# Blending the two softmax maps of a differential head before the transpose

## The reference, cut to what matters

```
def probs(qf, kf):
    s = einsum('bhqd,bhkd->bhqk', q_block, kf) * scale
    return softmax(where(mask, s, -inf), axis=-1)

a = probs(q1, k1) - lam * probs(q2, k2)
out = einsum('bhqk,bhkv->bhqv', a, v)
diff = rms_norm(out, diff_subln_g) * (1.0 - lam_init)
```

## The time and the profile before

| | us |
|---|---|
| median of three runs | 1382.27 (1382.13 to 1384.47) |
| the profiled execution, time | 1386.45 |
| the profiled execution, span | 1384.7 |
| TensorE busy | 1294.9 (94%) |
| VectorE busy | 844.6 (61%) |
| ScalarE busy | 648.8 (47%) |
| GpSimd busy | 145.3 (10%) |

### The profile page before, as it was taken

The page is one execution under the profiler, slowest core; times in us unless marked ns, Lnnn a source line. Parts: engine busy times, 40 slices in busy tenths (PEclk is TensorE's granted clock), DMA queues, the critical chain, the costliest instruction groups (busy, mean ns, idle before and its releaser), DMA issues.

```text
span 1384.7 us, 17635 instructions
## 1 busy us (share of the span) xinstructions
PE 1294.9 (94%) x6496; PEld 1084.3 (78%) x6496; DVE 844.6 (61%) x1011; ACT 648.8 (47%) x937; POOL 145.3 (10%) x161
## 2 busy tenths in 40 slices
PE   6979799999897989999997998999999999899997
PEld 5868688888686868888886887777899778688886
DVE  4588765455556896545445654667665586555454
ACT  4455454444344563544444253465564754444443
POOL 2927000000057430000000000000000000000000
PEclk9999999999988999999998989999999999999999
DMA  6512346556243314555553354233324445354551
GB/s 219 185 61 93 122 167 220 195 192 203 77 182 120 119 52 154 212 183 190 195 191 131 142 193 157 91 137 110 122 105 168 143 162 198 146 218 182 184 203 53
DMA packets 33683, 213.75 MB, mean 154 GB/s; under 512 B 4272, under 2 KB 6320, under 8 KB 9296
## 3 DMA queue, kind: packets, MB, share of 16 engines
q1 hardware_dynamic: 33552, 212.73, 43.0%
q0 software_dynamic: 64, 0.13, 0.0%
HBM read 211.80 MB, written 1.05 MB: 154 GB/s over the span
## 4 chain that ended last, share of the span: by engine, by line
PE 79%; DVE 12%; ACT 3%; issue 3%; POOL 2%; DMA 0%; DVEq 0%; SPq 0%; ACTq 0%; POOLq 0%; another core or an unknown queue 0%
PE bank L529 22%; PE bank L530 22%; PE bank L531 22%; PE bank L833 3%; DVE wlo L1472 2%; PE bank L642 2%; PE bank L610 2%; PE bank L560 1%; PE bank L629 1%; DVE index L1560 1%; ACT whi L1054 1%; PE bank L702 1%; DVE probs L1596 1%; PE bank L940 1%; POOL gain L453 1%
## 5 line engine op out<-in xcount | busy, mean ns | idle before, releaser
L1472 DVE TENSOR_TENSOR wlo<-raw,whi 128x2048 fp32r<-128x2048 f32 (+2 forms) x202 | 448.8, 2228 | 257.2 <-ACT whi L1054 255.7
L529 PE MATMUL bank<-whi,hT_hi 128*128 128x512 f32 (+2 forms) x1064 | 428.8, 403 | 20.7 <-DVE hT_lo L1496 14.3
L1054 ACT ACTIVATE whi<-raw 128x2048 fp32r<-128x2048 f32 (+2 forms) x202 | 370.7, 1842 | 114.9 <-PE bank L531 112.9
L530 PE MATMUL bank<-wlo,hT_hi 128*128 128x512 f32 (+2 forms) x1064 | 419.5, 394 | 0.0
L531 PE MATMUL bank<-whi,hT_lo 128*128 128x512 f32 (+2 forms) x1064 | 419.0, 394 | 0.0
L529 PEld LDWEIGHTS bank<-whi,hT_hi 128*128 128x128 f32 x1064 | 207.9, 195 | 66.4 <-issue 14.9
L531 PEld LDWEIGHTS bank<-whi,hT_lo 128*128 128x128 f32 x1064 | 207.6, 195 | 43.0
L530 PEld LDWEIGHTS bank<-wlo,hT_hi 128*128 128x128 f32 x1064 | 208.0, 195 | 39.0
L529 PE MATMUL bank<-whi,ffT_hi 128*128 128x512 f32 x240 | 93.7, 390 | 0.0
L531 PE MATMUL bank<-whi,ffT_lo 128*128 128x512 f32 x240 | 93.5, 390 | 0.0
L530 PE MATMUL bank<-wlo,ffT_hi 128*128 128x512 f32 x240 | 93.4, 389 | 0.0
(11 more groups left out here) (243 smaller groups left out, 1419.0 us busy)
## 6 DMA issues: line engine op xcount, KB each, us to landing
raw<-in_ff_loop SPq DMA_DIRECT2D x90, 1024.0 KB, 4.7
raw<-in_w_groups SPq DMA_DIRECT2D x77, 1024.0 KB, 4.8
raw<-in_w_out SPq DMA_DIRECT2D x8, 1024.0 KB, 4.7
raw<-in_ff_first SPq DMA_DIRECT2D x6, 1024.0 KB, 4.7
raw<-in_w_comp SPq DMA_DIRECT2D x4, 1024.0 KB, 4.7
raw<-in_ff_last SPq DMA_DIRECT2D x3, 1024.0 KB, 6.7
raw<-in_next_first SPq DMA_DIRECT2D x4, 512.0 KB, 3.7
raw<-in_next_first SPq DMA_DIRECT2D x2, 1024.0 KB, 4.7
```

Source lines behind the costliest of these rows:

```text
L529: eng.matmul(out, lhsT=hi, rhs=wh, start=start, stop=False)
L530: eng.matmul(out, lhsT=hi, rhs=wl, start=False, stop=False)
L1054: eng.activation(whi[j][:, 0:n], raw[j][:, 0:n], ACT.Copy).then_inc(hi_ready, 1)
L1472: eng.tensor_tensor(wlo[j][:, 0:n], raw[j][:, 0:n], whi[j][:, 0:n].bitcast(F32), ALU.subtract).then_inc(lo_ready, 1)
```

## The change

VectorE now combines the even and the odd map of each head into one map, before the transpose. It multiplies the odd map with the coefficient (even sum) x (-lam) / (odd sum) and adds the even map, which leaves the division by the even sum for the output. Only the combined map is transposed (6 tiles instead of 12) and multiplied with the values (6 tile products instead of 12), all into bank 5. ScalarE copies one bank of transposed maps instead of two, VectorE half a bank instead of one. The output needs one scaling instruction of 512 elements instead of four of 256 and a subtraction. `lam` is negated once a layer by one more small instruction.

TensorE's two waits for `o_done` ahead of `turn_heads` go, since bank 6 isn't written by the values any more. The transposes of a differential group no longer wait for the exponentials but for the new semaphore `blended`, which VectorE raises twice a group.

In this diff `blend`, the shown `blend_copy` and `diff_out` are VectorE's, `blend_turn` and `blend_values` TensorE's; ScalarE's own `blend_copy` is a copy of 512 columns after the first four tiles of a group's transposes.

```diff
+        coef = sb("coef", [P, 4])
+        blended = sem("blended")
...
+            def blend_turn(A, d):
+                eng.wait_ge(blended, 2 * d + 1)
+                for n in range(2):
+                    mm = eng.transpose(bank[2][:, n * P:(n + 1) * P], probs[:, 0, n * P:(n + 1) * P], ident[:, :])
+                eng.wait_ge(blended, 2 * d + 2)
+                for kt in range(2):
+                    for n in range(2):
+                        c = n * SEQ + kt * P
+                        out = bank[2][:, (2 + n) * P:(3 + n) * P] if kt == 0 else bank[3][:, n * P:(n + 1) * P]
+                        mm = eng.transpose(out, probs[:, 1, c:c + P], ident[:, :])
+                    mm.then_inc(pT_ready, 2 - kt)
+            def blend_values(A, c0):
+                eng.wait_ge(pT_act, 2 * A + 4)
+                eng.wait_ge(pT_dve, A + 2)
+                eng.wait_ge(o_done, A + 2)
+                for r in range(RT):
+                    for n in range(2):
+                        v = c0 + n * P
+                        for kt in range(r + 1):
+                            b = 2 * (r + kt) + n
+                            mm = eng.matmul(bank[5][:, (2 * r + n) * P:(2 * r + n + 1) * P],
+                                            lhsT=probsT[:, b // 4, b % 4 * P:(b % 4 + 1) * P],
+                                            rhs=z[:, kt, v:v + P], start=(kt == 0), stop=(kt == r))
+                mm.then_inc(pv_ready, 1)
...
-                attend_turn(A)
+                blend_turn(A, 2 * l)
...
-                attend_turn(A + 1)
-                eng.wait_ge(o_done, A + 3)
+                blend_turn(A + 1, 2 * l + 1)
                 turn_heads(l, 4, zcols(MQ), 4)
...
+            def blend(A, par):
+                eng.wait_ge(exped, 3 * A + 3)
+                dve(eng.reciprocal(inv[:, :], sums[:, par, :]))
+                dve.wait(eng)
+                even, odd = (a[:, :].rearrange("p (n two) -> p n two", two=2)[:, :, i] for i, a in ((0, sums[:, par]), (1, inv)))
+                dve(eng.scalar_tensor_tensor(out=coef[:, :], in0=even, scalar=lam[:, 0:1], in1=odd, op0=ALU.mult,
+                                             op1=ALU.mult))
+                dve.wait(eng)
+                for r in range(RT):
+                    for n in range(2):
+                        if r == 0:
+                            p, q = (probs[:, 0, (2 * n + i) * P:(2 * n + i + 1) * P] for i in range(2))
+                            out = probs[:, 0, n * P:(n + 1) * P]
+                        else:
+                            p, q = (probs[:, 1 + i, n * SEQ:(n + 1) * SEQ] for i in range(2))
+                            out = p
+                        c = 2 * r + n
+                        ins = eng.scalar_tensor_tensor(out=out, in0=q, scalar=coef[:, c:c + 1], in1=p, op0=ALU.mult,
+                                                       op1=ALU.add)
+                        if n:
+                            ins.then_inc(blended, 1)
+                        else:
+                            dve(ins)
+                            if r == 0:
+                                dve.wait(eng)
+            def blend_copy(A):
+                eng.wait_ge(pT_ready, 3 * A + 3)
+                eng.wait_ge(pv_ready, A + 1)
+                eng.tensor_copy(probsT[:, 1, 0:2 * P], bank[3][:, 0:2 * P]).then_inc(pT_dve, 1)
+            def diff_out(A):
+                eng.wait_ge(pv_ready, A + 2)
+                W = 2 * HD
+                eng.tensor_tensor(scr[:, 0, :].rearrange("p (n d) -> p n d", d=W),
+                                  bank[5][:, :].rearrange("p (n d) -> p n d", d=W),
+                                  inv[:, :].rearrange("p (n two) -> p n two", two=2)[:, :, 0:1].to_broadcast([P, 4, W]),
+                                  ALU.mult).then_inc(o_done, 1)
+                eng.wait_ge(o_done, A + 3)
...
-                lo(6, 0); copy_z1(t0, 5, MQ); lo(6, 1)
-                attend_copy(A)
+                lo(6, 0)
+                blend(A, 0)
+                copy_z1(t0, 5, MQ); lo(6, 1)
+                blend_copy(A)
...
-                diff_out(A, 0); diff_norm(l, 0)
+                diff_out(A); diff_norm(l, 0)
+                blend(A + 1, 1)
                 copy_z1(t0, 6, SQ); lo(7, 1)
-                attend_copy(A + 1)
+                blend_copy(A + 1)
```

More of the change, by code:

```diff
@@ L638, in attend_values @@
                     for h in range(4):
-                        out = bank[5][:, (4 * r + h) * dv:(4 * r + h + 1) * dv] if dv == HD else \
-                            bank[5 + r][:, h * dv:(h + 1) * dv]
+                        out = bank[5][:, (4 * r + h) * dv:(4 * r + h + 1) * dv]
                         for kt in range(r + 1):
@@ L779, in _ @@
                 attend_scores(A + 2, lambda h: T_MQ + h // 2, lambda h: T_MK + h // 2)
-                attend_values(A + 1, lambda kt, h: z[:, kt, DV + (2 + h // 2) * 2 * HD:DV + (3 + h // 2) * 2 * HD], 2 * HD)
+                blend_values(A + 1, DV + 2 * P)
                 project(7, 1)
                 attend_turn(A + 2)
-                eng.wait_ge(o_done, A + 4)
                 turn_heads(l, 5, zcols(SQ), 4)
@@ L1131, in attend_copy @@
                     eng.activation(probsT[:, u, :], bank[2 + u][:, :], ACT.Copy).then_inc(pT_act, 1)
+            def blend_copy(A):
+                eng.wait_ge(pT_ready, 3 * A + 2)
+                eng.wait_ge(pv_ready, A + 1)
+                eng.activation(probsT[:, 0, :], bank[2][:, :], ACT.Copy).then_inc(pT_act, 2)
             def diff_stats(l, i):
@@ L1534, in lambda_value @@
                 dve.wait(eng)
+                dve(eng.tensor_scalar(lam[:, 0:1], lam[:, 0:1], -1.0, None, ALU.mult))
+                dve.wait(eng)
             def head_sums(l, s):
@@ L1619, in attend_out @@
                         dve(ins)
-            def diff_out(A, par):
-                eng.wait_ge(pv_ready, A + 2)
+            def blend(A, par):
+                eng.wait_ge(exped, 3 * A + 3)
                 dve(eng.reciprocal(inv[:, :], sums[:, par, :]))
                 dve.wait(eng)
-                odd = inv[:, :].rearrange("p (n two) -> p n two", two=2)[:, :, 1:2]
-                dve(eng.tensor_scalar(odd, odd, lam[:, 0:1], None, ALU.mult))
+                even, odd = (a[:, :].rearrange("p (n two) -> p n two", two=2)[:, :, i] for i, a in ((0, sums[:, par]), (1, inv)))
+                dve(eng.scalar_tensor_tensor(out=coef[:, :], in0=even, scalar=lam[:, 0:1], in1=odd, op0=ALU.mult,
+                                             op1=ALU.mult))
@@ L1628, in diff_out @@
                 dve.wait(eng)
-                W = 2 * HD
                 for r in range(RT):
[L1631 to L1638, removed]
+                    for n in range(2):
[10 more added lines that the diff above has]
+                            ins.then_inc(blended, 1)
@@ L1639, in diff_out, with blend_copy @@
                         else:
                             dve(ins)
-                dve.wait(eng)
-                dve(eng.tensor_tensor(scr[:, 0, :], scr[:, 0, :], scr[:, 1, :], ALU.subtract))
-                dve.wait(eng)
+                            if r == 0:
+                                dve.wait(eng)
+            def blend_copy(A):
+                eng.wait_ge(pT_ready, 3 * A + 3)
+                eng.wait_ge(pv_ready, A + 1)
+                eng.tensor_copy(probsT[:, 1, 0:2 * P], bank[3][:, 0:2 * P]).then_inc(pT_dve, 1)
@@ L1773, in _ @@
                 attend_mask(A + 2, causal)
-                diff_out(A + 1, 1)
+                diff_out(A + 1)
                 attend_copy(A + 2)
```

2 lines of the change are left out of this document (1 added, 1 removed).

## The result

| | before | after |
|---|---|---|
| median of 5 runs of each, us | 1384.47 (1382.13 to 1389.08) | 1398.57 (1397.06 to 1400.86) |
| profiled execution, us | 1386.45 | 1398.18 |
| its span, us | 1384.7 | 1396.4 |
| mean granted clock of TensorE | 0.963 | 0.956 |
| TensorE busy, us | 1294.9 | 1295.8 |

The ratio is 1.0105, 95% interval 1.008 to 1.0129: the kernel is slower, by about twice as much as I forecast, and the time lies above my range (1384.5 to 1393.8). The direction and the place are as predicted, one term is not.

What follows compares the result with a forecast made beforehand. TensorE and VectorE were both taken to be near their limit, handing work to each other. Waits +3.3, clock falls +3.3 and GpSimd collision +1.1 gave +7.7 us on the median 1382.27: 1390.0 us, range 1384.5 to 1393.8.

Steps and rivals of the forecast that it cites:

- The direction and the place: Slower, at 82%; from group A's scores to the mixed rows' transposes (L560), longer by 2 to 5 us a layer.
- The first blend's second signal: Group A, layer 0: VectorE's signal for four of six transposes, at 104.85 us; projection 6 then starts +2.38 us.
- VectorE waits for the transposes of A+2: Behind the second blend VectorE, late before, becomes early and waits some 2 us for TensorE's transposes.
- VectorE's own sum: Both differential groups: blends add 3.9 us, output and copies save 5.2, so -1.3 us a layer.
- The half throughput rule: Rival, 3%: the blends' instructions with two non-bfloat16 SBUF sources run at half throughput, 3.2 us more, 1393.2 us.
- My terms without the clock: TensorE's waits for the two blends, +1.66 us a layer (+3.3 in all), and the GpSimd collision, +1.1 in all.
- The full collision: At `lo(7, 0)`, behind GpSimd's L459: up to 1.1 us lost; half taken in two layers, +1.1 in all.
- I count one fall a layer: TensorE's clock falls behind the A+1 pause only: 3.3 us at half speed lose 1.65 a layer, +3.3 in all.
- the 3.3 us that I had read at 838: Fall in the profile before: after 2.45 us of waiting at 838, clock at 0.53 for some 3.3 us.
- the first pause: TensorE's wait for group A's blend, about 3.3 us (101.5 to 105.0) with two transposes in it; no fall counted.
- The rival: The clock falls in both pauses of a layer: +6.6 us for the falls, +11 in all, 1393.3 us; chance 14%.
- the zero: Base of the forecast: the difference was put on the median of 1382.27 us, not the profiled execution's 1386.45.

Runs made afterwards that it cites:

- fill_both: The kernel after, with TensorE filling its waits for the blends of groups A (16) and A+1 (30) with transposes of the identity; ratio 1.0032 to before, 1390.21 us.
- early_both2: The kernel after, blend of A ahead of `lo(6, 0)`, blend of A+1 behind A's output but ahead of `lo(7, 0)` and the norm; ratio 0.9971 to before, 1382.29 us.
- early2_fill: early_both2 with 36 transposes of the identity in TensorE's wait ahead of the mixed rows; ratio 0.9987 to before, 1384.61 us.
- fill_first: The kernel after with only the wait of group A filled, with 16 transposes of the identity; ratio 1.0092 to before, 1398.4 us.
- early_a: The kernel after with only the blend of group A moved, ahead of `lo(6, 0)`; ratio 1.0036 to before, 1389.76 us.

## Why the prediction was wrong, point by point

**Right: what waits for what.** TensorE waits for the blend four times, and the other engines follow as I wrote. The first blend's second signal was predicted for 104.85; the transposes behind it start at 105.70, less 0.8 and the 0.13 of the way 104.77. VectorE waits for the transposes of A+2 (2.94 us; I said some 2), and the wait of 4.34 us ahead of the mixed rows is as it was: both engines were moved by the same amount.

**Right: VectorE's instructions.** Blend to next instruction: 105.56 - 103.62 = 1.94 and 127.24 - 125.29 = 1.95, predicted 1.96. The output takes 122.48 - 121.77 = 0.71, predicted 0.72. VectorE's own sum is 3.89 - (3.47 - 0.71) - (2.67 - 0.71) - 0.53 for the copies = -1.4 us a layer, predicted -1.3. The half throughput rule of the Trainium skill ("Vector Engine (DVE) Microarchitecture Reference", section 7) is denied by this trace: the four instructions with two float32 sources in SBUF, 768 elements in all, take 1.53 us.

**Right: waits and GpSimd.** My terms without the clock were 1.66 a layer and half of 1.1, 4.4 us in all; without falls of the clock fill_both measured 2.39 and 2.30 a layer and 0.32% of 1386 us, 4.4. The full collision of 1.05 was in it, so the waits come to 1.3 rather than 1.66, and that the sums agree is in part luck. In the kernel after the collision was 2.85 - 2.29 = 0.56, by chance of the alignment just the half that I took. The rule of the Trainium skill that I named with it ("SBUF — State Buffer", "Who interferes with whom") agrees with the 3.34 us of fill_both, where GpSimd was first.

**Wrong: "I count one fall a layer, behind the longer pause: +3.3 in all."** It is one term of the sum, mis-sized by a factor of two to three. Falls came behind all four pauses, and one of them lasted twice as long as the 3.3 us that I had read at 838. TensorE was busy at 1.2 GHz for 16.1 us, which is 8 us of work lost. The stretch shows 3.65 + 2.32 = 6.0 of it, the medians 1.0105 - 1.0032 = 0.73%, 10 us (roughly 6 to 14 by the two intervals). How it runs through the kernel is seen step by step in layer 0, each time less 0.8. Projection 6 starts at 105.67, +2.64 for the predicted +2.38. The masks of A+1 are at 114.23, +3.90 for +2.38, since 3.3 us of that projection ran at half speed. The blend of A+1 starts at 124.49 instead of 122.51. Projection 7 starts at 129.05 instead of 126.15, for this and since the transposes and heads behind the pause take 2.6 us instead of 1.6. The transposes of A+2 come at 145.35 instead of 140.98, and the mixed rows 6.04 later for 1.66.

What misled me: I held the first pause for too short, with "after 1.74 us it doesn't fall" as its other side. That left everything between 1.74 and 2.45 open, and the pauses of A, with two transposes in them, lay there. The other profiles fill in that very place of the third layer (L948; in the kernel after it is L975): behind single pauses of 1.40 to 1.84 us (eight profiles) the clock stayed at 1.00, behind 1.90, 1.96 and 1.97 us (early_both2, early2_fill, the kernel after) it fell. That holds for this place only: elsewhere the same pause had both outcomes, as said below. The kernel after:

```profile
886.76 1.42 PE L975 MATMUL bank<-ident,probs 128*128 128x128 f32 x8 [1.97 <-DVE probs L2137]
...
888.00:890.00 2.00, 2.00 (x6) 1.62 (x6) 2.00 (x2) 1.34 (x2) 0.00 (x0) 0.50 0.28 115
```

The rival was short in the same way: I gave two falls a layer 14% at 1393.3, and even that case took each fall for 3.3 us.

**Small: the zero.** I put the difference on a median of three runs, 1382.27. Beside the kernel after its median was 1384.47, and with 22 to 25 runs it is at 1384.95 to 1385.98. On 1384.47 the forecast would have been 1392.2, on the profiled execution's 1386.45 it would have been 1394.2; both are still too low.

**Open.** The stretch explains 10.7 us of the kernel after, the medians say 14 to 15. For fill_first it is 8.2 against 12.7, for early_a 2.0 against 5.0. The profiles show why it may be so: falls of the clock elsewhere come and go. The kernel before has none where the kernel after has one at 914 to 919, behind the same two pauses (1.22 and 1.31 us), and it has one at 397 to 405, with TensorE busy throughout and no pause in the 9 us ahead, where the kernel after has none. Added up over the whole profile, again in steps of 1 us, TensorE was busy at 1.2 GHz for about 76 us before, 91 after and 70 in fill_both; the last two differ by 21 us, which is 10 us of work, and their spans by 9.5. Executions of one kernel differ in the same way: the 25 of the kernel before that the last three runs were timed beside took 1381.7 to 1383.7 us at a mean clock of 0.965 and 1385.4 to 1386.9 at 0.963. Whether the changed stretch makes such falls likelier further on, no run here tells. I also can't say what makes the clock fall or not behind one and the same pause.

## What to carry to other kernels

When a change puts a new step of another engine between two steps of the one that is the path, work out the second signal's time first: here 8 us less matmul and 2.8 less vector work made 14 us more, and the same work, started a few microseconds sooner in the same stream, made 4 us less. Price each new pause of a dense TensorE as the wait plus a fall of its clock behind it, unless another engine is the path behind it; here a fall cost 1.0 to 2.8 us. One pause of about that length without a fall in the profile is no proof, as the same 3.59 us had both outcomes. Before filling such a pause to keep the clock up, look at which engine is the path behind it: only there is a higher clock time.

## What the runs showed of the hardware

- The granted clock was at the 1.2 GHz level behind a pause of 1.98 us, two transposes and 0.35 us more (layer 1 of the kernel after, clock 0.59 in the window of 2 us behind it). TensorE had been dense ahead of it.
- The same pause of 3.59 us in the same code had a fall behind it in one layer and none in the other (0.51 and 1.00).
- In one execution of the kernel after (layer 0), the fall behind the first pause took 3.3 us of TensorE's busy time, the one behind the second 6.3.
- The clock can fall without a pause: in the kernel before it was at the 1.2 GHz level from 397 to 405 us, with TensorE busy without a gap from 388 us on, the last 4 us before the fall with products of 128x72.
- With transposes of the identity in the pauses, of which nobody uses the result, the clock stayed at 1.00 behind them (fill_both). With such fills at two other places the mean clock rose to 0.973, and the time of the kernel before did not move (1.0009).
- A VectorE instruction of 2.29 us became 3.34 when a GpSimd instruction had started 0.09 us ahead of it, and 2.85 in another alignment.
